# Gates over all second keys in one pass, during the last 60 tiles of the up pass of an expert layer

## What is computed

```python
def block(xb):                                   # 256 tokens, D = 1024
    ...                                          # scores against two sets of 128 keys
    best_s, best_c = lax.top_k(cand.reshape(TOK_BLOCK, PEER_HEADS, K * K), K)
    i1 = jnp.take_along_axis(top_i[:, :, 0], best_c // K, axis=-1)
    i2 = jnp.take_along_axis(top_i[:, :, 1], best_c % K, axis=-1)
    e = (i1 * PEER_NKEYS + i2).reshape(TOK_BLOCK, PEER_HEADS * K)
    gate = jax.nn.softmax(best_s, axis=-1).reshape(TOK_BLOCK, PEER_HEADS * K)
    act = jax.nn.gelu(jnp.einsum('td,ted->te', xb, expert_u[e]), approximate=False)
    coef = (gate * act.astype(jnp.float32)).astype(xb.dtype)
    return jnp.einsum('te,ted->td', coef, expert_v[e])
```

## Time and profile before

| | us |
|---|---|
| median of 3 runs | 1799.74 |
| lowest and highest | 1796.98, 1811.25 |
| the profiled execution | 1801.02 |
| its span, first to last instruction | 1799.2 |
| TensorE busy in it | 1625.5 (90%) |
| DVE busy | 1123.3 (62%) |
| ACT busy | 773.6 (43%) |
| POOL busy | 473.7 (26%) |
| mean granted TensorE clock | 0.949 of full |

### The profile page before, as it was taken

How to read it: one execution, slowest core, us unless ns; L and a number is a source line. 1 busy time by engine, 2 the same in 40 slices (tenths; PEclk the granted TensorE clock), 3 DMA queues, 4 the chain that set the end, 5 groups by cost and what they waited for, 6 DMA issues and landing times.

```text
span 1799.2 us, 32624 instructions
## 1 busy us (share of the span) xinstructions
PE 1625.5 (90%) x11880; PEld 1478.1 (82%) x11880; DVE 1123.3 (62%) x1793; ACT 773.6 (43%) x1203; POOL 473.7 (26%) x235
## 2 busy tenths in 40 slices
PE   6988789997994777788899999999999999999998
PEld 5965689996993665578899999999998888888886
DVE  3366366565358566675428898656667777775554
ACT  3455455554443111124446566544332333335554
POOL 1210112221231221012222323433333333332322
PEclk8997899999997899789999999999998999999999
DMA  6540235553451000014445555544442444446654
GB/s 217 187 133 1 94 106 185 186 176 117 131 167 54 1 2 1 2 60 151 133 150 177 172 187 175 164 141 146 144 140 94 141 139 135 136 139 198 187 196 154
DMA packets 66240, 234.70 MB, mean 130 GB/s; under 512 B 8216, under 2 KB 9256, under 8 KB 66176
## 3 DMA queue, kind: packets, MB, share of 16 engines
q1 hardware_dynamic: 65776, 232.25, 39.8%
q0 software_dynamic: 400, 1.59, 0.2%
HBM read 232.74 MB, written 1.06 MB: 130 GB/s over the span
## 4 chain that ended last, share of the span: by engine, by line
PE 57%; issue 30%; DVE 7%; POOL 3%; ACT 2%; DMA 0%; SPq 0%; POOLq 0%; DVEq 0%; ACTq 0%
PE psum L673 25%; PE psum L1130 18%; PE psum L1095 6%; PE psum L687 3%; POOL w_lo L488 3%; PE psum L949 2%; DVE big L1387 1%; DVE w_lo L488 1%; DVE big L1401 1%; ACT w_hi L474 1%; PE psum L661 1%; DVE big L1428 0%; DMA big<-rel 0%; DVE x_hi L1656 0%; DVE big L1456 0%
## 5 line engine op out<-in xcount | busy, mean ns | idle before, releaser
L673 PE MATMUL psum<-x_hi,w_hi 128*128 128x256 f32 (+1 forms) x2192 | 628.9, 287 | 44.3 <-DVE x_lo L1193 23.3
L673 PE MATMUL psum<-x_lo,w_hi 128*128 128x256 f32 (+1 forms) x2192 | 623.4, 284 | 0.0
L673 PE MATMUL psum<-x_hi,w_lo 128*128 128x256 f32 (+1 forms) x2192 | 623.0, 284 | 0.0
L488 POOL TENSOR_TENSOR w_lo<-ring,w_hi 128x1024 fp32r<-128x1024 f32 x144 | 363.7, 2526 | 939.9 <-ACT w_hi L474 939.9
L488 DVE TENSOR_TENSOR w_lo<-ring,w_hi 128x1024 fp32r<-128x1024 f32 x290 | 366.1, 1263 | 247.1 <-ACT w_hi L474 246.4
L474 ACT ACTIVATE w_hi<-ring 128x1024 fp32r<-128x1024 f32 x434 | 456.1, 1051 | 86.0 <-PE psum L673 47.7
L673 PEld LDWEIGHTS psum<-x_hi,w_hi 128*128 128x128 f32 x2192 | 420.4, 192 | 50.5 <-issue 31.3
L673 PEld LDWEIGHTS psum<-x_hi,w_lo 128*128 128x128 f32 x2192 | 420.4, 192 | 0.0
L673 PEld LDWEIGHTS psum<-x_lo,w_hi 128*128 128x128 f32 x2192 | 418.4, 191 | 0.0
L1130 PE MATMUL psum<-w_hi,h_hi 128*128 128x512 f32 x512 | 164.4, 402 | 0.0
L2045 ACT ACTIVATE h_hi<-big 128x256 fp32r (+1 forms) x128 | 53.3, 417 | 250.6 <-PE psum L1130 243.1
(11 more groups left out here) (297 smaller groups left out, 2004.2 us busy)
## 6 DMA issues: line engine op xcount, KB each, us to landing
ring<-experts SPq DMA_DIRECT2D x256, 512.0 KB, 3.3
ring<-w_ffn SPq DMA_DIRECT2D x66, 512.0 KB, 3.4
ring<-w_in SPq DMA_DIRECT2D x46, 512.0 KB, 3.6
ring<-w_mid SPq DMA_DIRECT2D x24, 512.0 KB, 3.3
ring<-w_out SPq DMA_DIRECT2D x16, 512.0 KB, 4.0
ring<-w_q SPq DMA_DIRECT2D x16, 512.0 KB, 3.6
ring<-w_cmp SPq DMA_DIRECT2D x8, 512.0 KB, 3.3
big<-bias_rows POOLq DMA_DIRECT2D x1, 1536.0 KB, 8.6
```

The lines of the kernel that those rows point to most:

```text
L488: eng.tensor_tensor(w_lo[:, n % RING, :], ring[:, n % RING, :], w_hi[:, n % RING, :].bitcast(F32), ALU.subtract).then_inc(low_ready2 if n ...
L673: mm = pe.matmul(dst, w[:, slot, k * P:(k + 1) * P], x[:, k, t0:t0 + width], start=(n == 0), stop=(n == 3 * len(chunks) - 1))
```

## The change

- A quad now covers all 128 second keys: `hot_2` is [choice, 4 tokens, 128 keys], a matmul is 128x128, and one PSUM bank holds one quad. `keys(q)` makes `hot_2` and `hot_1` together, always two quads ahead. There are 64 quads and none in the down pass.
- The up pass runs its last 60 tiles in four trips of 15 tiles and 16 quads (two behind the 15th).
- The gates of a quad multiply `act_all` for all 128 second keys at once, also those whose tile is still to come. POOL therefore fills the columns of tiles 68 to 127 with ones beforehand (`fill`: eight pieces between its splits of tiles 2 to 25, four and one of 3600 columns after the choice is made). From tile 68 on, ACT writes the Gelu into one of three buffers (`fresh`), and POOL (`evict`, 256 columns) multiplies it into the column block, which by then holds ones, and gates for the tokens that had their turn.
- `evict(e)` waits for the Gelu of `e` and for `gated_acts` of all quads before the one behind tile `e`; `gated_acts(q)` waits for the quad's matmuls and for `evict` of the tile that it stands behind (`fresh_used`); the Gelu of `e` waits for `evict(e - 3)`. TensorE's tile `e` waits for the Gelu of `e - 2`.

```diff
+        hot_1 = (by_four(flat2(h_hi[:])), by_four(flat2(h_lo[:])))
+        hot_2 = (by_four(sqf[:, 0:4 * P]), by_four(sqf[:, 4 * P:8 * P]))
+        fresh = (kept_sb[:, ones_at:ones_at + TX], kept_sb[:, ones_at + TX:ones_at + 2 * TX], rms[:, 0:TX])
+        gate_bank = lambda q: psum[:, 6 + q % 2, :].rearrange("p (e t) -> p e t", t=4)
         act_all = big[:, :].rearrange("p (e t) -> p e t", e=NE)
...
-            pool_splits(B_MID + 10, B_EXP + E0 + 2)
+            pool_splits(B_MID + 10, B_EXP + 2)
+            pool.sem_inc(fresh_used, 3)
+
+            def fill(at, n):
+                pool.memset(big[:, at:at + n], 1.0).then_inc(ones_filled, 1)
+
+            SCORE0 = NE * TX - 7696
+            FILLED = [(a, min(1024, SCORE0 - a)) for a in range(E0 * TX, SCORE0, 1024)]
+            for c, (a, n) in enumerate(FILLED):
+                fill(a, n)
+                pool_splits(B_EXP + 2 + 3 * c, B_EXP + 5 + 3 * c)
...
+            pool.wait_ge(pick_shift, 2)
+            for c in range(4):
+                fill(SCORE0 + 1024 * c, 1024)
+            pool_splits(B_EXP + 62, B_EXP + E0 + 1)
+            pool.wait_ge(chosen_ready, 2)
+            fill(SCORE0 + 4096, 3600)
...
+            def weigh(q, i=None):
+
+                at = 4 * q if i is None else i * (4 * GQ) + 4 * q
+                pool.wait_ge(hot_2_raw, trip(q + 1, i, GQ))
+                pool.tensor_tensor(hot_2[q % 2], hot_2[q % 2], chosen_t[:, 0, bass.ds(at, 4)].unsqueeze(2).to_broadcast([P, 4, NE]),
                                    ALU.mult).then_inc(hot_2_ready, 1)
...
+            def evict(e, q, i=None):
+                pool.wait_ge(expert_act, trip(BODY + e + 1, i, GT))
+                pool.wait_ge(gates_used, trip(q + 2, i, GQ))
+                a = act_all[:, trip(e, i, GT), :]
+                pool.tensor_tensor(a, a, fresh[(e - E0) % 3], ALU.mult).then_inc(fresh_used, 1)
+
+            def up_pool(k, b, i=None, last=False):
+                split_low(pool, B_EXP + E0 + b * GT + k + 2, i, (2,), GT)
+                evict(E0 + b * GT + k, b * GQ + k, i)
+                for q in (k, k + 1)[:1 + k // (GT - 1)]:
+                    if not last or q + 2 < GQ:
+                        weigh(b * GQ + q + 2, i)
+
+            split_low(pool, B_EXP + E0 + 1, None, (2,))
             weigh(0)
-            for j in range(GB):
-                up_pool(j)
-            with pool.Fori(0, (NE - E0) // GB - 1) as i:
-                for j in range(GB):
...
+            weigh(1)
+            with pool.Fori(0, TRIPS - 1) as i:
+                for k in range(GT):
+                    up_pool(k, 0, i)
+            for k in range(GT):
+                up_pool(k, TRIPS - 1, last=True)
+            pool_splits(B_V + 2, N_TILES)
...
+            def gated_up(e, i=None):
+                slot = tile_split(pe, B_EXP + e, i, GT)
+                pe.wait_ge(expert_act, trip(e + BODY - 1, i, GT))
+                project(slot, psum[:, (e - E0) % 5, 0:TX], TX).then_inc(tiles_used, 1)
+
...
+                pe.wait_ge(hot_1_ready, trip(q + 1, i, GQ))
+                pe.wait_ge(hot_2_ready, trip(q + 1, i, GQ))
+                pe.wait_ge(gates_used, trip(q + 1, i, GQ))
                 for t in range(4):
-                    mm = pe.matmul(bank[:, 4 * (q % 2) + t, :], hot_1_read(q)[:, t, :], hot_2(g)[:, 4 * (q % 2) + t, :],
+                    mm = pe.matmul(gate_bank(q)[:, :, t], hot_1[q % 2][:, t, :].bitcast(F32), hot_2[q % 2][:, t, :],
                                    start=True, stop=True)
                 mm.then_inc(gates_done, 1)
...
+            with pe.Fori(0, TRIPS) as i:
+                for k in range(GT):
+                    gated_up(E0 + k, i)
+                    four_gates(k, i)
+                four_gates(GT, i)
...
+            pieces(B_V, NE - 2, pe, expert_down)
...
+            def keys(q, i=None):
+
+                at = 4 * q if i is None else i * (4 * GQ) + 4 * q
+                iota4 = const("iota").unsqueeze(1).to_broadcast([P, 4, NE])
+                dve.tensor_tensor(hot_2[q % 2], iota4, chosen_t[:, 2, bass.ds(at, 4)].unsqueeze(2).to_broadcast([P, 4, NE]),
+                                  ALU.is_equal).then_inc(hot_2_raw, 1)
+                dve.tensor_tensor(hot_1[q % 2], iota4, chosen_t[:, 1, bass.ds(at, 4)].unsqueeze(2).to_broadcast([P, 4, NE]),
                                   ALU.is_equal).then_inc(hot_1_ready, 1)
...
+            def gated_acts(q, k, b, i=None):
+                at = 4 * q if i is None else i * (4 * GQ) + 4 * q
+                dve.wait_ge(gates_done, trip(q + 1, i, GQ))
+                dve.wait_ge(fresh_used, trip(3 + b * GT + min(k, GT - 1) + 1, i, GT))
+                a = act_all[:, :, bass.ds(at, 4)]
+                dve.tensor_tensor(a, gate_bank(q), a, ALU.mult).then_inc(gates_used, 1)
+
+            def up_dve(k, b, i=None, last=False):
+                split_low(dve, B_EXP + E0 + b * GT + k + 2, i, per=GT)
+                for q in (k, k + 1)[:1 + k // (GT - 1)]:
+                    gated_acts(b * GQ + q, q, b, i)
+                    if not last or q + 2 < GQ:
+                        keys(b * GQ + q + 2, i)
...
             dve.sem_inc(gates_used, 2)
-            second_keys(0)
...
+            keys(1)
+            dve.wait_ge(ones_filled, 4 + 1 + (NE * TX - 7696 - E0 * TX + 1023) // 1024)
+            dve.wait_ge(expert_act, BODY + E0)
+            with dve.Fori(0, TRIPS - 1) as i:
+                for k in range(GT):
+                    up_dve(k, 0, i)
+            for k in range(GT):
+                up_dve(k, TRIPS - 1, last=True)
...
+            pieces(B_V, NE - 3, dve, second)
...
+            def fresh_expert(e, i=None):
+                split_high(act, B_EXP + e + 2, i, GT)
+                act.wait_ge(tiles_used, trip(B_EXP + e + 1, i, GT))
+                act.wait_ge(fresh_used, trip(e - E0 + 1, i, GT))
+                act.activation(fresh[(e - E0) % 3], psum[:, (e - E0) % 5, 0:TX], ACT.Gelu).then_inc(expert_act, 1)
+
+            with act.Fori(0, TRIPS) as i:
+                for k in range(GT):
+                    fresh_expert(E0 + k, i)
```

More of the change, by code:

```diff
@@ L1110, in _ @@
             expert_up(E0 - 1)
[L1112 to L1117, removed]
+            with pe.Fori(0, TRIPS) as i:
[3 more added lines that the diff above has]
+                four_gates(GT, i)
             pe.wait_ge(expert_act, BODY + NE)
-            pe.wait_ge(gates_used, 2 + GROUPS)
+            pe.wait_ge(gates_used, 2 + QUADS)
             for tt in range(2):
@@ L1660, in second_keys @@
-            def second_keys(g, i=None):
-                if g >= 2:
-                    dve.wait_ge(gates_done, trip(2 * g - 2, i, GB))
-                t0 = 8 * (g % GROUPS)
-                at = t0 if i is None else i * (4 * GB) + t0
-                e0 = KEPT["iota"][0] + HALF * (g // GROUPS)
-                dve.tensor_tensor(hot_2(g), kept_sb[:, e0:e0 + HALF].unsqueeze(1).to_broadcast([P, 8, HALF]),
-                                  chosen_t[:, 2, bass.ds(at, 8)].unsqueeze(2).to_broadcast([P, 8, HALF]),
-                                  ALU.is_equal).then_inc(hot_2_raw, 1)
@@ L1671, in gated_acts @@
-            def gated_acts(g, i=None):
-                t0 = 8 * (g % GROUPS)
-                at = t0 if i is None else i * (4 * GB) + t0
-                e0 = HALF * (g // GROUPS)
-                dve.wait_ge(gates_done, trip(2 * g + 2, i, GB))
-                a = act_all[:, e0:e0 + HALF, bass.ds(at, 8)]
-                dve.tensor_tensor(a, psum[:, gate_bank(g), :].rearrange("p (e t) -> p e t", t=8), a,
-                                  ALU.mult).then_inc(gates_used, 1)
-            def up_dve(j, i=None):
-                split_low(dve, B_EXP + E0 + j + 2, i, per=GB)
-                first_keys(j + 2, i)
-                if j % 2:
-                    second_keys((j + 1) // 2, i)
-                elif j:
-                    gated_acts(j // 2 - 1, i)
+            def keys(q, i=None):
[4 more added lines that the diff above has]
+                dve.tensor_tensor(hot_1[q % 2], iota4, chosen_t[:, 1, bass.ds(at, 4)].unsqueeze(2).to_broadcast([P, 4, NE]),
+                                  ALU.is_equal).then_inc(hot_1_ready, 1)
@@ L1688, in _ @@
             dve.sem_inc(gates_used, 2)
-            second_keys(0)
-            first_keys(0)
+            keys(0)
             split_low(dve, B_EXP + E0 + 1)
-            first_keys(1)
-            dve.wait_ge(expert_act, BODY + HALF)
-            for j in range(GB):
-                up_dve(j)
-            with dve.Fori(0, (NE - E0) // GB - 1) as i:
-                for j in range(GB):
-                    up_dve(GB + j, i)
-            second_keys(31)
-            first_keys(62)
-            gated_acts(29)
@@ L1702, in _ @@
-            first_keys(63)
-            gated_acts(30)
-            gated_acts(31)
+            keys(1)
[6 more added lines that the diff above has]
+                up_dve(k, TRIPS - 1, last=True)
             def low_coef(e, i=None, per=BODY):
@@ L1718, in second @@
```

(24 more changed lines are left out.)

74 lines of the change are left out of this document (10 added, 64 removed).

## The result

The changed kernel takes 1816.75 us (median of 20 runs, 1808.29 to 1825.41) against 1799.62 (20 runs, 1796.98 to 1811.25). The ratio of like runs is 1.0073, with a 95% interval of 1.0056 to 1.0090: 0.7% slower. The profiled execution took 1809.55, its span is 1807.8 against 1799.2. The times of both kernels lie in two groups some 7 us apart, and the two medians happen to fall in different ones; the lower groups (1797 to 1801 and 1808 to 1811) have medians 12.7 us apart, 1797.94 and 1810.65, and what follows goes by the traces.

A forecast was written before the change was run, and what follows sets the result against it. TensorE was taken to set the pace in all three passes. A loss of 82.0 us in the up pass less 69.8 gained in the down pass, +12.2, gave 1813.2 on the profiled 1801.02, less 1.3 for the median: 1812 us, range 1788 to 1850.

The forecast's parts named there:

- The ring: Gated up pass: waits between POOL and DVE make one lap per tile, 4.56 us with DVE's split, 6.00 with POOL's.
- Turns of DVE and POOL: Gated up pass: POOL `tensor_tensor` and DVE splits or keys exclude each other, overlapping 0.05 or 0.13 us; `gated_acts`, reading PSUM, is free.
- Start, second quads, end: Gated up pass, beside the laps: start 7.8 us, three second quads at 2.06 each (6.2), end 2.0.
- Down pass: Down pass without its 64 quads: tiles run plain at 2.70 us each, a gain of 69.8 us.
- The ones: POOL's fills before the gated tiles: expected to cost nothing, 15 us if each blocked DVE and TensorE waited.
- The sum: Whole kernel: +82.0 us in the up pass less 69.8 in the down pass, +12.2 us.
- The span of this case: Forecast case alone: 0.14 on `evict` is 8 us, 0.15 on the hand-over 9 us; stated span 1794 to 1838.
- TensorE about 75% busy: Sign expected in the changed profile: over tiles 68 to 127 TensorE waits for `w_lo`, with about 75% busy.
- Clock: Rival, gated up pass: TensorE drops to half clock, 7.54 us per tile and quad; 15 laps add 37 us, 1849; chance 0.11.
- No exclusion: Rival, gated up pass: DVE's keys and splits run beside POOL, laps 3.14 and 5.54 us, total 1750; chance 0.08.
- hidden links: Rival, gated up pass: only exclusive time counts, 265 us for the stretch, total 1764; chance 0.07.
- TensorE stays the bound at 3.77: Rival, gated up pass: no effective ring, TensorE sets the pace at 3.77 us per lap; no chance of its own given.

The follow-up runs named there:

- e1: Changed kernel with POOL's low splits of the gated up tiles moved to DVE; 1787.82 us (one run).
- e2: Changed kernel with POOL's `evict` of a tile placed ahead of its own split; 1799.80 us (one run).
- e3: Changed kernel with `evict` multiplying only 128 of its 256 columns; 1800.02 us (one run).
- e4: Changed kernel with the chosen second keys kept in PSUM, so key instructions read one SBUF operand instead of two; 1788.94 us (one run).
- e6: Changed kernel with second keys kept in PSUM and `evict` on DVE from PSUM; median 1727.04 us of 5, ratio 0.9589 to the kernel before.
- e8: Kernel before the change, without the 64 quads of its down pass (their keys, `weigh`, matmuls, `gated_acts`); 1729.45 us (one run).
- e7: Changed kernel with every fill of ones made twice; 1817.36 us (one run).
- e5: Changed kernel with Gelu written back to PSUM and `evict` done by DVE, not POOL; median 1754.97 us of 5, ratio 0.9722 to the kernel before.

## Why the prediction was right

The forecast was 1812 us, 0.7% slower; 1816.75 and 0.7% were measured. By its steps:

- *The ring.* Right in form and in size. Laps of 4.56 and 6.00 were worked out, 4.60 and 5.94 measured. `evict` was put at 0.66 and is 0.72 (0.73) alone, 0.06 more; its hand-over to DVE at 0.15 and is 0.13 to 0.16 in the looped trips and 0.10 to 0.11 in the last; the saving of a blocked `evict` at 0.05 and is 0.14, from 0.72 to 0.58; DVE's split behind `weigh` at 1.01 and is 1.09; POOL's split at 2.40 and is 2.35. The errors are of both signs and leave +0.04 and -0.06. e1, e2 and e3 each change one link, and the stage moves by 26.8, 17.5 and 16.4 us.
- *Turns of DVE and POOL.* Right, with its exemption for an operand in PSUM, which rested on one meeting in the earlier trace rows. e4 shows it as a change of one operand of the two key instructions, e6 at the size of the whole kernel.
- *Start, second quads, end.* The start was put at 7.8 and took 6.2 (1137.04 to the first `evict` at 1143.2), since the first keys are made at 1135.46, beside tile 67. A second quad was put at 2.06; it shows as 1.80 and then a lap of 6.23 instead of 5.94, together 2.09. The last `evict` to the last `gated_acts` took 3.1 (from 1444.8), not 2.0, its start being counted while it is blocked. All told 310.9 us against 312.4: a loss of 80.5, forecast 82.0.
- *Down pass.* 1798.68 - 1451.33 = 347.4 against 416.6, a gain of 69.2; forecast 69.8. e8 gives 68.3 from the other side.
- *The ones.* Put at nothing, and that is what they cost: tile 67 comes 195.30 us after the start of the up pass with and without them. As many again cost 1.5 us (e7), through the order on POOL and not through DVE. The last fill ends at 1134.85 and the first keys start at 1135.46, as foreseen. The Trainium skill, "SBUF — State Buffer", section "Who interferes with whom", says that a DVE instruction with two SBUF inputs contends with a GpSimd instruction that reads SBUF and not with one that only writes it; by that rule the fills cost nothing, and the two meetings under e7 agree.
- *The sum.* +80.5 - 69.2 = +11.3. The spans differ by 8.6. The other -2.6 lies ahead of the gates (the x48 piece starts at 1134.19, before at 1136.81). It is there already at the start of the up pass (938.64 and 941.27), and less than the spread of these points over the kernels. It isn't a part of the change.
- *The span of this case.* Its two swings, 8 us for `evict` and 9 us for the hand-over, give 1795 to 1829 around 1812; the 1838 that is stated has no term behind it. Nothing else goes by it.
- *TensorE about 75% busy.* It shows 84%. Matmul ends that no other follows count in full (a quad alone is 1.13 in the record, 0.89 in a row of work), and some tiles ran at the low clock. How the difference divides between the two wasn't worked out.

**The rivals.** *Clock.* It did fall, in short pieces, and cost nothing measurable. Over the stage (1137 to 1448) the granted clock is 0.96, which is some 25 us at the lower level by estimate (0.04 x 311 / 0.5), against 15 laps of 7.54 in the rival. The stretch with most of it:

```profile
1280.00:1290.00 10.00, 4.82 (x38) 4.30 (x36) 6.87 (x8) 1.86 (x3) 6.78 (x6) 0.90 0.31 105
1290.00:1300.00 10.00, 10.00 (x67) 10.00 (x68) 5.17 (x8) 1.33 (x2) 7.16 (x5) 0.75 0.17 54
1300.00:1310.00 10.00, 10.00 (x86) 9.84 (x85) 8.53 (x10) 3.99 (x6) 5.97 (x4) 1.00 0.37 120
```

A granted clock of 0.75 over 10 us is 5 us at the lower level of 1.2 GHz, behind a stretch in which TensorE was 48% busy. The tiles then take longer, but the ring doesn't wait for them: the laps on both sides of it are 4.60, 4.60 and 5.94, as between 1300 and 1350 at the full clock, and the second quad in it (1.80, then 6.23) is as long as at the end of the trip before. So the fall of the clock is there, and the "15 of the 60 laps" at half clock, one behind another, are not. *No exclusion* (3.14 and 5.54 per lap) and *hidden links* fall with the laps, and "TensorE stays the bound at 3.77" with the 167.81 of 200. That last is what e6 makes true.

## What to carry to other kernels

When a change puts a producer and a consumer of two engines into the same tile, write down the ring of waits (who must be done before whom, once around) and add it up with the turns that the two engines take; the busy shares, all under 85% here, say nothing about it. Then look for the link with the cheapest other place: moving one operand to PSUM gave back 19.8 us (e4), moving `evict` to the engine that waited for it 63.3 us (e5), and the two together the whole 80.5 us that the ring had cost, which made the change a gain of 4.1% (e6). Where a duration was above an operation's plain one here, the rest was time spent blocked, and a DVE at 99% had room (e5 to e6).

## What the runs showed of the hardware

- A blocked instruction loses less than the wait. `evict` behind DVE's split took 0.58 from the split's end, 0.72 alone. POOL's `weigh` behind a key took 0.97 from the start of DVE's next instruction, 1.04 alone.
- A POOL product of 256 columns took 0.72 and of 128 columns 0.45, so by a straight line through the two some 0.18 of it doesn't depend on the size (an estimate). A memset of 1024 columns took 0.95 and of 3600 columns 3.12, less than the 1.25 for 1024 that the one row before had given.
- Laps in looped trips were longer than in the last, written-out trip by 0.04 (4.60 and 4.56), and by 0.14 in e4. The rows put it into the hand-overs: POOL to DVE 0.13 to 0.16 against 0.10 to 0.11, DVE to POOL (e4) 0.17 against 0.08. What makes them longer was not tried.
